# A decoder trunk on one core: TensorE's first expert turn ahead of its loop, and GpSimd's drain, the sums' requests and the last bias moved

## The reference, cut to what matters

```python
def hierarchical_moe(h, wg, bg, we, be, w_gate, w_up, w_down):
    ...
    gate = g_p * jax.nn.softmax(e_top, axis=-1)
    expert = (g_idx * EXPERTS_PER_GROUP + e_idx).reshape(-1)
    y_pairs = grouped_expert_ffn(xf, expert, w_gate, w_up, w_down).reshape(n_tok, TOP_K_INNER, d)
    y = jnp.einsum('nkd,nk->nd', y_pairs, gate.astype(y_pairs.dtype))
...
        return (jax.nn.silu(xblk @ w_gate[e]) * (xblk @ w_up[e])) @ w_down[e]
...
        h = layer_norm(DN_ALPHA * h + f, ln_ffn_g[layer], ln_ffn_b[layer])
```

## Time and profile before

| what | value |
|---|---|
| time, median of 3 runs | 2789.59 us (2788.68 to 2796.17) |
| the profiled execution's own time | 2793.26 us |
| its span in the profile | 2791.5 us |
| TensorE matmuls, share of the span | 89% |
| VectorE / ScalarE / GpSimd | 73% / 61% / 23% |
| mean granted TensorE clock | 0.935 |
| first experts stage (e0), then c0 | 870.8 to 1575.0 us, then to 1616 us |
| second experts stage (e1), then c1 | 2071.2 to 2757.5 us, then to the end |

### The profile page before, as it was taken

One profiled execution on the slowest core, in us unless ns is written; L12 is line 12 of the kernel. 1 busy time (PEld: TensorE's weight loads), 2 busy tenths in 40 slices (PEclk: granted clock), 3 DMA queues, 4 the chain that ended last, 5 costly groups with the idle time before them and its releaser, 6 DMA issues. The chain is left out here.

```text
span 2791.5 us, 37703 instructions
## 1 busy us (share of the span) xinstructions
PE 2495.4 (89%) x12607; PEld 2117.0 (76%) x12607; DVE 2033.3 (73%) x2460; ACT 1706.9 (61%) x1831; POOL 651.5 (23%) x485
## 2 busy tenths in 40 slices
PE   8889987997895999999999589997969999999992
PEld 8779966876584788888888488986857888888882
DVE  4687775667667898888898545545468898888884
ACT  2367835655413677777777446564126777777773
POOL 0105616643000211221222312121001212222213
PEclk9899998997896999999999789998978999999996
DMA  5503233220535879998899411103246879999994
GB/s 168 123 1 95 72 94 91 83 56 9 159 97 216 309 249 366 368 373 290 292 370 358 154 61 38 38 23 123 91 166 244 322 262 370 365 368 365 376 351 143
DMA packets 115271, 565.12 MB, mean 202 GB/s; under 512 B 23520, under 2 KB 27872, under 8 KB 65904
## 3 DMA queue, kind: packets, MB, share of 16 engines
q1 hardware_dynamic: 89776, 512.15, 50.2%
q0 software_dynamic: 25408, 51.84, 6.9%
HBM read 574.22 MB, written 74.34 MB: 232 GB/s over the span
## 5 line engine op out<-in xcount | busy, mean ns | idle before, releaser
L1920 DVE TENSOR_TENSOR e0wlo<-e0raw,e0whi 128x2048 fp32r<-128x2048 f32 x214 | 486.6, 2289 | 68.8 <-ACT e0whi L1768 68.8
L1920 DVE TENSOR_TENSOR e1wlo<-e1raw,e1whi 128x2048 fp32r<-128x2048 f32 x208 | 472.8, 2288 | 67.0 <-ACT e1whi L1768 67.0
L1768 ACT ACTIVATE e0whi<-e0raw 128x2048 fp32r<-128x2048 f32 x214 | 409.9, 1916 | 103.4 <-PE e0u L90 43.4
L1768 ACT ACTIVATE e1whi<-e1raw 128x2048 fp32r<-128x2048 f32 x208 | 398.3, 1915 | 99.4 <-PE e1u L90 42.2
L88 PE MATMUL odd_ps<-h2T_hi,odd_w_hi 128*128 128x348 f32 x480 | 158.3, 330 | 6.2 <-DVE odd_w_lo L2371 6.2
L89 PE MATMUL odd_ps<-h2T_lo,odd_w_hi 128*128 128x348 f32 x480 | 155.6, 324 | 0.0
L90 PE MATMUL odd_ps<-h2T_hi,odd_w_lo 128*128 128x348 f32 x480 | 155.4, 324 | 0.0
L88 PE MATMUL m_y<-m_whi,m_xhi 128*128 128x512 f32 (+1 forms) x304 | 121.9, 401 | 23.3 <-DVE m_wlo L1503 22.8
L89 PE MATMUL m_y<-m_wlo,m_xhi 128*128 128x512 f32 (+1 forms) x304 | 120.4, 396 | 0.0
L90 PE MATMUL m_y<-m_whi,m_xlo 128*128 128x512 f32 (+1 forms) x304 | 120.1, 395 | 0.0
L88 PE MATMUL e0g<-e0whi,e0xh 128*128 128x512 f32 x284 | 116.3, 409 | 3.6 <-issue 3.6
(11 more groups left out here) (455 smaller groups left out, 7145.9 us busy)
## 6 DMA issues: line engine op xcount, KB each, us to landing
e0raw<-in_moe_w_gate SPq DMA_DIRECT2D x72, 1024.0 KB
e0raw<-in_moe_w_up SPq DMA_DIRECT2D x72, 1024.0 KB
e0raw<-in_moe_w_down SPq DMA_DIRECT2D x72, 1024.0 KB
e1raw<-in_moe_w_gate SPq DMA_DIRECT2D x70, 1024.0 KB
e1raw<-in_moe_w_up SPq DMA_DIRECT2D x70, 1024.0 KB
e1raw<-in_moe_w_down SPq DMA_DIRECT2D x70, 1024.0 KB
qki_w_raw<-in_w_even SPq DMA_DIRECT2D x22, 512.0 KB, 5.1
odd_w_raw<-in_w_odd SPq DMA_DIRECT2D x20, 512.0 KB, 3.6
```

The costliest lines, as they stand in the source:

```text
L1768: act.activation(w_hi[:, i, :], raw[:, i, :], ACT.Copy).then_inc(hi_done[i], 1)
L1920: dve.tensor_tensor(w_lo[:, i, :], raw[:, i, :], w_hi[:, i, :].bitcast(F32), ALU.subtract).then_inc(lo_done[i], 1)
```

## The change

There are four edits.

1. TensorE's list of `experts` makes turn 0 outside the loop: `up_turn(0)` and `transpose_x(2)` stand ahead of the wait for `by_slot`, `down(0)` behind it, and the loop runs from 1.
2. VectorE's first list makes `split_w(2, 1)` behind `split_x(1)`, `hidden(0)` and `slot_gates()` in place of ahead of them.
3. GpSimd has a drain between its last scatter and the wait for its landing. SyncE asks for the first two row blocks of the sums in `experts`, and for the others at the start of `combine`.
4. In c1 alone, ScalarE copies the bias to PSUM, and the last row block gets its bias from VectorE in place of GpSimd; its store waits for a semaphore of its own.

```diff
+BEFORE_CHANGE, BEHIND_CHANGE = slice(0, 2), slice(2, None)
...
-    def load_rows(self, sp):
-        for n, b in enumerate(self.blocks):
+    def load_rows(self, sp, part):
+        for n in range(len(self.blocks))[part]:
+            b = self.blocks[n]
...
-            sums.load_rows(sp)
+            sums.load_rows(sp, BEFORE_CHANGE)
...
                                     bounds_check=n_tok - 1, oob_is_err=False, compute_op=ALU.add).then_inc(y_stored, 16)
+            pool.drain()
             pool.wait_ge(y_stored, m * 16 + 32)
...
                 split_w(i, 1)
-            split_w(2, 1)
             split_x(1)
             hidden(0)
             slot_gates()
-            split_w(3, 1)
+            for i in WU:
+                split_w(i, 1)
...
             last.then_inc(by_slot_mm, 1)
+            up_turn(0)
+            transpose_x(2)
             pe.wait_ge(by_slot_done, 1)
+            down(0)
             m = blocks_but_two(pe)
-            with pe.Fori(0, m) as g:
+            with pe.Fori(1, m) as g:
                 turn(g)
...
         def _(sp):
+            sums.load_rows(sp, BEHIND_CHANGE)
             if beside is not None:
                 beside(sp)
...
-                sp.wait_ge(normed, n + 1)
+                if n < N - 1 or turned:
+                    sp.wait_ge(normed, n + 1)
+                else:
+                    sp.wait_ge(last_normed, 1)
...
                 dve.tensor_tensor(x(n), x(n), g, ALU.mult).then_inc(gained, 1)
+                if n == N - 1 and not turned:
+                    dve.wait_ge(gained, N)
+                    dve.wait_ge(bias_in, 1)
+                    dve.tensor_tensor(x(n), x(n), t_ps[0][:].rearrange("p a n -> p (a n)"), ALU.add).then_inc(last_normed, 1)
...
             act.activation(g_ps[:].rearrange("p a n -> p (a n)"), sums.gain(0), ACT.Copy).then_inc(gain_in, 1)
+            if not turned:
+                act.activation(t_ps[0][:].rearrange("p a n -> p (a n)"), sums.gain(1), ACT.Copy).then_inc(bias_in, 1)
...
-            for n in range(N):
+            n_here = N if turned else N - 1
+            for n in range(n_here):
```

More of the change, by code:

```diff
@@ L2120, in combine @@
         t_ps = [c.ps(name + f"t{s}", [P, 2, 512]) for s in range(TURN_SETS)]
-        stored = c.sem(name + "so")
+        stored, bias_in, last_normed = c.sem(name + "so"), c.sem(name + "bin"), c.sem(name + "lnd")
         chain, padded, gain_in, var_done, root_done, scales, centred, gained, normed, t_mm, hi_d, lo_d = (
@@ L2215, in _ @@
             pool.wait_ge(sums.gains_loaded, 32)
-            for n in range(N):
+            n_here = N if turned else N - 1
+            for n in range(n_here):
                 pool.wait_ge(gained, n + 1)
                 pool.tensor_tensor(x(n), x(n), sums.gain(1)[0:toks(blocks[n]), :], ALU.add).then_inc(normed, 1)
-            pool.wait_ge(normed, N)
+            pool.wait_ge(normed, n_here)
         if turned:
```

## The result

| kernel | median (us) | lowest to highest | runs |
|---|---|---|---|
| before | 2790.33 | 2788.68 to 2796.17 | 4 |
| after the change | 2773.56 | 2770.55 to 2777.10 | 4 |

The ratio is 0.9934, with a 95% interval of 0.9922 to 0.9947: 0.66% faster. The forecast was 2773.6 us, with a range of 2768 to 2781.

The account below looks back on a forecast made before the run. The prediction blamed TensorE's stalls before its loops, and drains and first instructions at stage ends. Gains of 9.0 (first turns), 2.7 (e0 to c0), 3.3 (e1 to c1) and 1.0 (end) make 16.0 us: 2789.59 to 2773.6, range 2768 to 2781.

Parts of the forecast that it names:

- The stalls go (3.6 and 4.4 us): TensorE's waits behind the 128x48 products, before the loop's first product in e0 and e1, vanish: 3.56 and 4.44 us.
- I take the loop's entry as hidden: TensorE's sequencer reads the turns' number and enters the loop behind down(0) at no cost; bounds 0 and 1.3 us per stage.
- So I keep one such loss, 1.73 us per stage.: Behind the small products in e0 and e1, TensorE's clock still falls, costing 1.73 us per stage.
- The first rival: TensorE's clock stays up in both first turns: 3.5 us more, 19.5 gained, 2770.1 us; chance 0.2.
- So this costs nothing either: SyncE asking for chunk 2 of turn 2 some 2.4 us later is free; at most 2.4 us lost per stage.
- 0.3 because the transposes (0.89 us in place of 0.60): In e1's first turn, transposes return to full clock: 0.3 us of the 5.4 gained there.
- Drain, number of DMAs: GpSimd's drain length goes with DMAs since the last drain, not the landing it follows: 82 to 85 ns each.
- With 6.01 us the drain ends at 1570.94: At e0's end the drain runs while the last scatter flies, ending at 1570.94 in place of 1574.01; 2.7 us gained.
- 3.3 us for e1: From e1 to c1, the earlier drain gains 3.3 us, VectorE's start being limited by the first rows' landing at 2754.2.
- 0.3 us late: c0's third row block, asked for only after the drain, lands at 1576.0 while VectorE wants it at 1575.7.
- The end, 1.0 us: At c1's end, one bias add fewer on GpSimd makes the last store land 1.0 us earlier; bounds 0.9 and 1.9.
- The slower rival: The loops become bound by weights, ScalarE waiting for DMA each turn: 2806 us at 0.5 us per turn; chance 0.04.

Follow-up runs that it names:

- first_turn_old_list: The changed kernel with VectorE's first list back in its old order: 2780.97 us, one run.
- old_bias: The changed kernel with GpSimd adding the last bias again and no copy of the bias to PSUM: 2770.38 us, one run.
- early_requests: early_drain with SyncE asking for the gate weights (WG) of turn 2 ahead of WD of turn 1: 2773.83 us, one run.
- no_drain: The changed kernel without its added GpSimd drain, requests still split: 2776.41 us, one run.
- after_again: The changed kernel itself measured once more, the second series: 2777.46 us, ratio 0.9949 to before, 6 runs.
- wait_ahead: The changed kernel with TensorE's wait for by_slot put back ahead of its first turn: 2775.53 us, one run.
- tail_alone: The kernel before with only the added drain, the split requests and the last-bias change: 2784.21 us, ratio 0.9975.
- first_turn_alone: The kernel before with only TensorE's first turn ahead of its loop and VectorE's list reordered: 2779.97 us, ratio 0.9959.
- early_drain: The changed kernel with the added drain moved ahead of the last but one scatter's issue: 2771.56 us, ratio 0.9939, 4 runs.

## Why the prediction was right, and where its steps were not

The sign, the time and the range were right: 2773.56 against 2773.6 us, and the second series' 2777.46 is also inside the range. That the first agrees to 0.1 us is luck: the first series gained 16.8 us by its medians and the second 12.6, where the sum had 16.0, terms were off in opposite directions, and the executions spread by more. By its steps:

- **The stalls go (3.6 and 4.4 us).** Right: both are gone in both profiles of the changed kernel (0.1 us at most stays), and first_turn_old_list shows that edit 2 is needed for it, else 1.66 and 1.42 us stay. The margin in e1 is thin: in old_bias and early_requests, which have both edits, TensorE still waits 0.7 and 0.6 us there for the tokens' low part.
- **"I take the loop's entry as hidden".** Right: no gap of 1.3 us behind `down(0)` in any kernel with edit 1.
- **"So I keep one such loss, 1.73 us per stage."** This step failed in its size. The reasoning behind it, that the row of small products and hardly idle time brings the fall, was half right. Counting the stages of all kernels with edits 1 and 2 that kept the row whole and did not wait for `by_slot` (seven kernels, 14 stages), the clock fell at the row's end in 2: in no_drain's e0 and after_again's e1, each without a stall. Two others of the 14 had a stall of 0.63 and 0.67 us (e1 of early_requests and old_bias) and no fall. In wait_ahead and first_turn_old_list, with stalls of 0.3 to 1.7 us behind the whole row, it fell in 4 of 4, once ahead of the stall. In before and tail_alone, with 3.4 us and more, it fell in 4 of 4, at most 0.6 us behind the row's end, and once 0.3 us ahead of it.

  The right term was the loss times a small chance, not the loss. The first rival (the clock stays up) describes the stages of the first profile. Its price, 3.5 us, was right for e1 alone: the stretch of the table takes 22.63 us with the fall (after_again) and 20.8 without. In e0 the one fall among these kernels cost nothing that can be seen: no_drain's e0 reached the first transpose 1.5 us later, but its first turn then took 18.1 us, with no wait of TensorE, and the whole stretch 22.34 us, in the midst of the 21.63 to 22.91 us of the five profiles of this kind in which the clock held (early_requests, with its other order of requests, left out). What the clock gives there, the wait for weights takes back (next point).

  The rule of the Trainium skill ("TensorE: Matmul & The Clock Gate", section "What's actually happening") that the clock follows recent activity agrees with the traces that have no stall and no fall; read as a rule on idle time alone it does not explain the falls at 914.60 (first_turn_old_list), 910.44 (no_drain), 2109.70 (after_again) and 2112.58 (tail_alone, whose row ends at 2112.89), which all came while TensorE was busy.
- **"So this costs nothing either" (chunk 2 of turn 2).** Failed for e0: its first turn takes 0.8 us more in after, 1.3 in after_again (19.43) and 1.8 in first_turn_alone (19.95). The bound of 2.4 us once per stage held. What I left out is that this stretch of e0 is bound by DMA: taking 5 us out of TensorE's time brings TensorE and ScalarE nearer to weights that can't land earlier. Where TensorE came later, by a stall or a fall (wait_ahead, first_turn_old_list, no_drain), the turn took 18.1 us again. The one other order tried, early_requests, made it worse. e1 has no such wait in either profile of the change.
- **"0.3 because the transposes (0.89 us in place of 0.60)".** Right, 0.60 us, together with the clock. e1's term of 5.4 became 7.3 us with the clock up and 5.5 with it down; e0's 3.6 became 4.6 and 3.9.
- **Drain, number of DMAs.** Right as to what it goes with: no_drain and early_drain show it. The ratios of 82 to 85 ns held in no_drain too (6012 / 73, 5859 / 71).
- **"With 6.01 us the drain ends at 1570.94", then 3.3 us for e1.** Right for e0 and wrong for e1. The forecast let the whole drain run from the scatter's issue on. In e0 it does, to 0.02 us in six profiles and 0.2 in the first: there half a drain ends just about when the scatter lands, so the second half has nothing to wait for, and 2.6 us were gained where 2.7 were foretold. In e1, whose scatter flies 1.4 us longer, the second half waits: the drain ended 2.95 us behind the landing, where the forecast had 1.5 (2751.96 less 2750.43). It put this wait at nothing, and 2.7 us were gained, not 3.3. The limit that I had named for it, the landing of the first rows, was not reached.
- **"0.3 us late" for c0's third row block.** 0.1 us: it was asked for at 1563.56 and landed at 1567.28, after 3.7 us, and VectorE took it at 1567.31. The estimate of 3.2 us from the Trainium skill ("DMA: Bandwidth & Descriptors", section "Anatomy of one DMA", whose fit is for DMAs issued by GpSimd) was half a microsecond short for these requests of SyncE.
- **The end, 1.0 us.** 0.7 us in both profiles, 0.8 by old_bias. The stores are as foretold (0.37 us apart, the last landing 3.6 us after its issue), but VectorE waits 0.16 us for the first root of c1, which ScalarE makes behind its added copy, and GpSimd's last adds start 22.44 us behind the first statistics in place of 22.19. The copy was to run beside a wait for the first rows, and that wait is not there.
- **The slower rival.** Nothing of it: in e1's loop ScalarE's longest wait is the same as in the earlier trace rows, and no entry for a DMA stands ahead of it.

```profile
ACT e1whi L1771 <- PE e1u L90: 40.8, 64, 0.9
```

## What stays open

Why the clock falls at a given moment is not settled: single executions point to both shares, but not to how they combine, and the same kernel fell in one execution and not in another. Nor is it shown what GpSimd's drain does in its two halves; that the second waits for the last landing is read from where 14 drains ended. The drain without the split of the requests was not run either. And whether early_drain is better than the change, by the 2 us that its two `combine` stages show, could not be told from times that spread over 10 us.

## What to carry to other kernels

When a drain stands at a stage's end, divide its length by the DMAs that the engine issued since the last one: if the quotient is the same in several stages, it can be paid earlier, where the engine is idle. Begun behind the last DMA's issue, half of it still has to wait for the landing. Take a wait off an engine's path only together with the list of the engine it waits for, and ask which transfer was just hidden by the time that goes: here 0.8 to 1.8 us of 5 came back as a wait for weights. And where single executions spread by more than the edit, compare stretches between named instructions, not totals.

## What was not expected of the hardware

- GpSimd's drain costs 82 to 85 ns per DMA since the last one, counted from the end of the engine's last instruction. Begun while the last scatter flies, at least half of it (3.0 us for 73 DMAs, 2.95 for 71) came behind the landing. With two DMAs it takes 217 ns.
- TensorE's granted clock fell to 0.50 in the midst of work on 128x48 products (914.60, 910.44), and held 1.00 through idle stretches of 1.52 and 1.75 us behind a row half as long.
- Two 512 KB stores 0.37 us apart: 2.6 us to land for the first, 3.6 for the second.
